# A two-layer hybrid decoder trunk in fp32r triple products: the two token halves of a projection unit computed side by side

## The chip, the cores and the metric

One Trainium2 chip, one core. The metric is the device time of one execution in microseconds; the number given for a kernel is the median of its runs.

## The reference

x is 1024 tokens by 1024 features, fp32. Two layers, then a final RMSNorm:

```python
def hybrid_layer(x, p_i, ...):
    h = rmsnorm(x, norm_mix)
    z = h @ w_in                        # 1024 x 3336: retention, pooling, mLSTM inputs
    ...                                 # y_ret, y_pool, y_ml: chunkwise mixing over tokens
    x = x + concat([y_ret, y_pool, y_ml]) @ w_out
    h = rmsnorm(x, norm_ffn)
    gu = h @ w_gate_up                  # 1024 x 5632
    x = x + (silu(gu[..., :D_FF]) * gu[..., D_FF:]) @ w_down    # D_FF = 2816
    hp = rmsnorm(x, norm_ple)
    x = x + sigmoid(hp @ w_ple_gate) * (p_i @ w_ple_proj)
    return x
```

## The kernel before

Activations are kept transposed: features on the 128 partitions in eight blocks, tokens along the free dimension in two halves of 512 (HALF), h = 0 and 1. The residual is `x`; the normed input of a projection is split into `h_hi` and `h_lo` (both fp32r), each weight tile into `w_hi` and `w_lo`, and a product is three matmuls of 128x128 by 128x512: w_hi with h_hi, w_lo with h_hi, w_hi with h_lo (`three_passes`, lines 1300 to 1302). Each `pe.matmul` loads its own stationary tile; the trace lists the loads as PEld.

The weights come in units of 128x1024 (111 per layer). SP loads a unit (512 KB) into one of two raw buffers, GpSimd splits it with two instructions (w_hi, L1285; w_lo, L1288) into a ring of three, when TensorE has reported the unit three places back as done (`unit_done`).

A narrow unit is one block of 128 outputs over all eight input blocks: two fills, one for each token half, of 8 x 3 = 24 matmuls. A wide unit (down projection and p_i @ w_ple_proj) is four blocks of 128 outputs over two input blocks: eight fills of 2 x 3 = 6 matmuls, in the order block 0 half 0, block 0 half 1, block 1 half 0 and so on. Each fill goes to the next of four PSUM banks of the tile `proj`. Before a fill TensorE waits until the bank's former content is read (`emptied`, one count for each bank), after its last matmul it increments `fill_done` or, for the unit's last fill, `unit_done` (`tell`). The other four banks (`aux`) serve the mixing work.

Readers of the fills: the input projections are scaled by rstd into SBUF (VectorE L516). In the conv stage (units 1 to 6) VectorE then runs the causal convolution (L528, L531) and row work of the mLSTM gates between the units. Output and down projections are added to x (VectorE L854, `add_fill`). In an up stage (four units: gate, up, gate, up) VectorE scales the gate unit (L866), ScalarE takes silu, VectorE scales the up unit (L873), multiplies (L878), ScalarE copies to act_hi (L1219), VectorE subtracts to act_lo (L883). Within a unit VectorE goes half 0, half 1: L873 and L878 for half 0, then for half 1, then L883 for both. The ple gate: L995, sigmoid on ScalarE, L1000, L1003 (adds to x), L442 (adds the square).

The engines' programs are fixed sequences in the order of MACRO. The FFN: up(group 0), then for each further group up(g), down(g - 1), at last down(10). So an up stage is followed by a down stage 10 times a layer. During the output projection and the last down stage VectorE also adds ScalarE's squares (L442) and makes h_lo (`low_part`, L431) for the next norm: in the output projection the eight blocks of half 0 come after fill 14, those of half 1 after fill 15; TensorE's first fill of the next unit waits for them block by block (h_ready). The rstd of the norm is applied after the projection, so it is wanted only by the readers of the fills.

Of the kernel before, what the change touches and what calls it, by code (L numbers as in the profile page):

```python
# [29 lines left out]
P = 128  # L30
D = 1024
S = 1024
HALF = 512
DEPTH = 2
KC = D // P
# [173 lines left out]
def build(nc, w_d, x_d, p_d, pos_d, const_d, par_d, early_d, out_d):  # L209
    spill_d = nc.dram_tensor("x_spill", (P, KC, S), F32, kind="Internal").ap()  # L210
    with ExitStack() as ctx:
# [1081 lines left out]
        def _(pe):  # L1293
# [30 lines left out]
            def wide(L, u, k, rhi, rlo, fills=0, units=0):  # L1324

                if k == 0:
# [4 lines left out]
                             lambda c: rhi[:, c, hs(h)], lambda c: rlo[:, c, hs(h)]), u, k)  # L1331

            def sums(L, base, i):

                for h in range(2):
                    pe.wait_ge(sq_added.sem, sq_added.at(L, base + 15 + h))
                    pe.wait_ge(aux_read(("sum", i, h)), aux_free_at(L, ("sum", i, h)))
                    for t in range(4):
                        ins = pe.matmul(aux[:, h, t:t + 1], acc[:, h, P * t:P * t + P], const[:, C_PART:C_PART + 1],
                                        start=True, stop=True)  # L1340
                    ins.then_inc(aux_done.sem, 1)
# [12 lines left out]
            with pe.Fori(0, DEPTH) as L:  # L1354
                for item in MACRO:
                    what, args = item[0], item[1:]
                    if what == "unit":
                        u = args[0]
                        for h in range(2):
                            ready = None  # L1360
# [191 lines left out]
                    elif what == "out_units":  # L1552
# [9 lines left out]
                        for m in range(2, 8):  # L1562
                            for h in range(2):
                                narrow(L, U_OUT + m, h)
                    elif what == "ffn":
                        def up(u, g, lp, first=False):
                            for f in range(4):
                                for h in range(2):
                                    ready = None
# [9 lines left out]
                        def down(u, g, lp):  # L1579
                            pe.wait_ge(act_ready.sem, act_ready.at(L, lp.acts + (4 * g + 4)))  # L1580
                            for k in range(16):
                                wide(L, u + k // 8, k % 8, ahi[:, g % 2], alo[:, g % 2], lp.fills, lp.units)

# [16 lines left out]
                    elif what == "ple_gate":  # L1600
                        for m in range(8):
                            for h in range(2):
                                ready = None
                                if m == 0:
                                    ready = lambda i, k, h=h: pe.wait_ge(h_ready.sem, h_ready.at(L, 48 + 8 * h + k + 1))
                                narrow(L, U_GATE + m, h, ready=ready)
# [135 lines left out]
```

## Time and profile before

| | |
|---|---|
| runs | 2929.11, 2934.57, 2944.49 us; median 2934.57 us |
| span of the profiled execution | 2929.3 us, mean granted TensorE clock 0.984 |
| PE (matmul) busy | 2767.3 us, 94%, 12804 matmuls |
| PEld (weight loads) busy | 2242.3 us, 77%, 12804 loads |
| DVE / ACT / POOL busy | 1572.0 us (54%) / 479.7 us (16%) / 1011.8 us (35%) |
| chain that ended last | PE 80%, DVE 11%, issue 6%, ACT 2% |
| projection matmuls, per line 1300, 1301, 1302 | 2784 from h, 704 from act, 64 from p |

How to read it: PE is TensorE, DVE is VectorE, ACT is ScalarE, POOL is GpSimd. A matmul's record (0.39 us) reaches over the start of the next one, so busy time says that TensorE is seldom idle, and start-to-start distances say how fast it goes.

### The profile page before, as it was taken

To read this page: it belongs to the slowest core of one execution; us is meant where nothing else is said; L and a number is where in the kernel's file an instruction comes from. 1 tells how busy PE (TensorE), PEld (TensorE's weight loads), DVE (VectorE), ACT (ScalarE), POOL (GpSimd) and SP (SyncE) were. 2 spreads that over 40 slices of the span, in tenths; PEclk is the share of its full clock that TensorE was granted. 3 is DMA by queue.
4 is the path that set the end of the run, shared out by engine and by line. 5 is a ranking of instruction groups with operands and counts; after the bars stand their busy time and mean duration, and the time that the engine had idled before them with its cause. 6 is when DMAs were issued, how large, how long until landed. Compare 5 with 4: busy or idle time off the path is not lost.

```text
span 2929.3 us, 34599 instructions
## 1 busy us (share of the span) xinstructions
PE 2767.3 (94%) x12804; PEld 2242.3 (77%) x12804; DVE 1572.0 (54%) x2098; ACT 479.7 (16%) x719; POOL 1011.8 (35%) x449
## 2 busy tenths in 40 slices
PE   3899999999999999999978999999999999999997
PEld 3678876778888888787866887668888878888875
DVE  5957844454334334446768677345433444433566
ACT  4020212230000000004221001142200000000232
POOL 2432311333434343344433222204343434343441
PEclk9999999999999999999989999999999999999998
DMA  5110001111111111111121001021111111111111
GB/s 188 44 37 30 30 29 65 65 44 51 43 50 43 50 50 43 50 43 44 51 95 37 30 30 37 29 80 58 44 44 50 43 50 43 50 44 49 50 42 60
DMA packets 38027, 147.49 MB, mean 50 GB/s; under 512 B 4384, under 2 KB 4640, under 8 KB 36512
## 3 DMA queue, kind: packets, MB, share of 16 engines
q1 hardware_dynamic: 31968, 116.41, 11.9%
q10 hardware_dynamic: 5952, 29.65, 2.7%
q8 instruction: 68, 1.11, 0.2%
q14 instruction: 39, 0.32, 0.0%
HBM read 132.94 MB, written 12.58 MB: 50 GB/s over the span
## 4 chain that ended last, share of the span: by engine, by line
PE 80%; DVE 11%; issue 6%; ACT 2%; DVEq 0%; ACTq 0%; DMA 0%
PE proj L1300 24%; PE proj L1302 24%; PE proj L1301 24%; DVE ml_qk L531 2%; PE aux L1532 1%; PE aux L1533 1%; DVE mix L542 1%; DVE h_lo L431 1%; PE aux L1413 1%; DVE square_sum L442 1%; DVE x L854 1%; PE aux L1445 1%; PE aux L1434 1%; PE aux L1503 1%; PE aux L1471 1%
## 5 line engine op out<-in xcount | busy, mean ns | idle before, releaser
L1300 PE MATMUL proj<-h_hi,w_hi 128*128 128x512 f32 x2784 | 1105.2, 397 | 83.8 <-DVE h_lo L431 61.3
L1301 PE MATMUL proj<-h_hi,w_lo 128*128 128x512 f32 x2784 | 1091.7, 392 | 0.0
L1302 PE MATMUL proj<-h_lo,w_hi 128*128 128x512 f32 x2784 | 1091.4, 392 | 0.0
L1285 POOL TENSOR_TENSOR w_hi<-w_raw,zero 128x1024 fp32r<-128x1024 f32 x222 | 437.8, 1972 | 1845.8 <-PE proj L1302 1839.0
L1300 PEld LDWEIGHTS proj<-h_hi,w_hi 128*128 128x128 f32 x2784 | 527.8, 190 | 200.8 <-DVE h_lo L431 62.5
L1301 PEld LDWEIGHTS proj<-h_hi,w_lo 128*128 128x128 f32 x2784 | 527.7, 190 | 110.9 <-issue 3.3
L1302 PEld LDWEIGHTS proj<-h_lo,w_hi 128*128 128x128 f32 x2784 | 527.1, 189 | 111.5
L1288 POOL TENSOR_TENSOR w_lo<-w_raw,w_hi 128x1024 fp32r<-128x1024 f32 x222 | 573.9, 2585 | 17.4
L854 DVE TENSOR_TENSOR x<-x,proj 128x512 f32<-128x512 f32 x384 | 257.5, 685 | 221.5 <-PE proj L1302 221.0
L1300 PE MATMUL proj<-act_hi,w_hi 128*128 128x512 f32 x704 | 278.2, 395 | 23.2 <-DVE x L854 23.2
L1302 PE MATMUL proj<-act_lo,w_hi 128*128 128x512 f32 x704 | 276.9, 393 | 0.0
L1301 PE MATMUL proj<-act_hi,w_lo 128*128 128x512 f32 x704 | 274.8, 390 | 0.0
L873 DVE TENSOR_TENSOR act<-proj,rstd 128x512 f32<-128x512 f32 x88 | 60.9, 692 | 372.1 <-PE proj L1302 372.1
L866 DVE TENSOR_TENSOR silu_g<-proj,rstd 128x512 f32<-128x512 f32 x88 | 60.4, 688 | 275.9 <-PE proj L1302 275.9
L1215 ACT ACTIVATE silu_g<-silu_g 128x512 f32<-128x512 f32 x88 | 55.4, 632 | 748.4 <-DVE silu_g L866 748.4
L1300 PEld LDWEIGHTS proj<-act_hi,w_hi 128*128 128x128 f32 x704 | 132.3, 188 | 58.9 <-DVE x L854 31.8
L1302 PEld LDWEIGHTS proj<-act_lo,w_hi 128*128 128x128 f32 x704 | 132.3, 188 | 29.2
L1301 PEld LDWEIGHTS proj<-act_hi,w_lo 128*128 128x128 f32 x704 | 132.2, 188 | 29.2
L883 DVE TENSOR_TENSOR act_lo<-act,act_hi 128x512 fp32r<-128x512 f32 x88 | 153.5, 1782 | 0.0
L1219 ACT ACTIVATE act_hi<-act 128x512 fp32r<-128x512 f32 x88 | 55.7, 633 | 490.5 <-DVE act L878 490.5
L1026 ACT ACTIVATE squares<-x 128x512 f32<-128x512 f32 x112 | 70.3, 631 | 257.7 <-DVE x L854 175.1
L878 DVE TENSOR_TENSOR act<-act,silu_g 128x512 f32<-128x512 f32 x88 | 107.6, 1223 | 6.1
(192 smaller groups left out, 1972.1 us busy)
## 6 DMA issues: line engine op xcount, KB each, us to landing
w_raw<-weights SPq DMA_DIRECT2D x222, 512.0 KB, 3.2
x_spill<-x ACTq DMA_DIRECT2D x2, 4096.0 KB, 12.5
x<-x_spill ACTq DMA_DIRECT2D x4, 1536.0 KB, 7.2
x<-x_in ACTq DMA_DIRECT2D x8, 512.0 KB, 11.2
out<-x ACTq DMA_DIRECT2D x16, 256.0 KB, 3.0
x<-x_spill ACTq DMA_DIRECT2D x2, 1024.0 KB, 4.9
p_raw<-p_in ACTq DMA_DIRECT2D x2, 1024.0 KB, 5.0
const<-constants ACTq DMA_DIRECT2D x1, 1241.0 KB, 16.7
```

What stands on the lines that cost most here:

```text
L531: v.scalar_tensor_tensor(dst, r[:, t:t + S], w[t], dst, ALU.mult, ALU.add).then_inc(vec_step.sem, 1)
L854: v.tensor_tensor(x[:, m, hs(h)], x[:, m, hs(h)], pbank(u, k), ALU.add).then_inc(emptied[bank(u, k)].sem, 1)
L866: v.tensor_tensor(silu_g[:, h, :], pbank(ug, h), rstd[:, h, :], ALU.mult).then_inc(emptied[bank(ug, h)].sem, 1)
L873: v.tensor_tensor(act_t[:, h, :], pbank(uu, h), rstd[:, h, :], ALU.mult).then_inc(emptied[bank(uu, h)].sem, 1)
L878: v.tensor_tensor(act_t[:, h, :], act_t[:, h, :], silu_g[:, h, :], ALU.mult).then_inc(act_made.sem, 1)
L883: v.tensor_tensor(alo[:, g % 2, f, hs(h)], act_t[:, h, :], ahi[:, g % 2, f, hs(h)].bitcast(F32), ALU.subtract).then_inc(act_ready.sem, 1)
L1026: a.activation(sqr[:, j % 2, :], x[:, c, hs(h)], ACT.Square).then_inc(sq_made.sem, 1)
L1285: g.tensor_tensor(whi[:, slot, :], w, zero1[:, 0:1].to_broadcast([P, 1024]), ALU.add).then_inc(w_hi_made, 1)
L1288: g.tensor_tensor(wlo[:, slot, :], w, whi[:, slot, :].bitcast(F32), ALU.subtract).then_inc(weights_ready.sem, 1)
L1300: pe.matmul(out, wh, rhi, start=first, stop=False)
L1301: pe.matmul(out, wl, rhi, start=False, stop=False)
L1302: return pe.matmul(out, wh, rlo, start=False, stop=final)
```

## The change

A new helper `both` computes the two token halves of one block together: for each input block w_hi is used for half 0 and for half 1, then w_lo for both, then w_hi for both with h_lo, so that consecutive matmuls write alternate banks, and each stationary tile is loaded two times running. `narrow_both` and `wide_both` wait for the weights and for both banks before the first matmul, and report both fills at the end. They take the place of `narrow` and `wide` in the whole units of the input projection from unit 2 on, output units 2 to 7, the up units (but the first two of a layer), the down units and gate units 1 to 7. All sums, their order within a bank, the number of matmuls and loads, and the programs of the other engines are as before.

```diff
+            def both(L, u, ks, outs, rhi, rlo):
+
+                last = len(ks) - 1
+                for i, (k, wk) in enumerate(ks):
+                    wh, wl = whi[:, u % RING, wk:wk + P], wlo[:, u % RING, wk:wk + P]
+                    for h in range(2):
+                        pe.matmul(outs[h], wh, rhi(k, h), start=i == 0, stop=False)
+                    for h in range(2):
+                        pe.matmul(outs[h], wl, rhi(k, h), start=False, stop=False)
+                    ends = [pe.matmul(outs[h], wh, rlo(k, h), start=False, stop=i == last) for h in range(2)]
+                return ends
+
+            def narrow_both(L, u, fills=0, units=0):
+
+                pe.wait_ge(weights_ready.sem, weights_ready.at(L, units + (u + 1)))
+                for h in range(2):
+                    pe.wait_ge(emptied[bank(u, h)].sem, free_at(L, u, h, fills))
+                ends = both(L, u, [(k, P * k) for k in range(KC)], [pbank(u, 0), pbank(u, 1)],
+                            lambda k, h: hh[:, k, hs(h)], lambda k, h: hl[:, k, hs(h)])
+                for h in range(2):
+                    tell(ends[h], u, h)
+
+            def wide_both(L, u, m, rhi, rlo, fills=0, units=0):
+
+                if m == 0:
+                    pe.wait_ge(weights_ready.sem, weights_ready.at(L, units + (u + 1)))
+                for h in range(2):
+                    pe.wait_ge(emptied[bank(u, 2 * m + h)].sem, free_at(L, u, 2 * m + h, fills))
+                ends = both(L, u, [(0, P * m), (1, HALF + P * m)], [pbank(u, 2 * m), pbank(u, 2 * m + 1)],
+                            lambda c, h: rhi[:, c, hs(h)], lambda c, h: rlo[:, c, hs(h)])
+                for h in range(2):
+                    tell(ends[h], u, 2 * m + h)
...
-                        for h in range(2):
+                        if u > U_GATES + 1:
+                            narrow_both(L, u)
+                        for h in range(2 if u <= U_GATES + 1 else 0):
...
                         for m in range(2, 8):
-                            for h in range(2):
-                                narrow(L, U_OUT + m, h)
+                            narrow_both(L, U_OUT + m)
...
                             for f in range(4):
-                                for h in range(2):
+                                if not (first and f < 2):
+                                    narrow_both(L, u + f, lp.fills, lp.units)
+                                for h in range(2 if first and f < 2 else 0):
...
-                            for k in range(16):
-                                wide(L, u + k // 8, k % 8, ahi[:, g % 2], alo[:, g % 2], lp.fills, lp.units)
+                            for m in range(8):
+                                wide_both(L, u + m // 4, m % 4, ahi[:, g % 2], alo[:, g % 2], lp.fills, lp.units)
...
                         for m in range(8):
-                            for h in range(2):
+                            if m > 0:
+                                narrow_both(L, U_GATE + m)
+                            for h in range(2 if m == 0 else 0):
```

## Rows read from the trace of the kernel before

**Rows 1.** Grouped instructions: line, engine, out<-in, shapes, count | busy us, mean ns | idle before

```profile
L1300 PE MATMUL proj<-h_hi,w_hi 128*128 128x512 f32 x2784 | 1105.2, 397 | 83.8 <-DVE h_lo L431 61.3 <-DVE conv_raw L516 22.2 <-DVE ml_v L516 0.3
```

**Rows 2.** Timeline of TensorE, narrow units: start us, duration us, engine, line, operation

```profile
1213.29 0.39 PE L1301 MATMUL proj<-h_hi,w_lo 128*128 128x512 f32 x1
1213.52 0.39 PE L1302 MATMUL proj<-h_lo,w_hi 128*128 128x512 f32 x1
1213.75 0.39 PE L1300 MATMUL proj<-h_hi,w_hi 128*128 128x512 f32 x1
```

**Rows 3.** Timeline of TensorE, last up matmul and first down fills, with weight loads

```profile
1235.28 0.39 PE L1302 MATMUL proj<-h_lo,w_hi 128*128 128x512 f32 x1
...
1236.67 0.39 PE L1302 MATMUL proj<-act_lo,w_hi 128*128 128x512 f32 x1
...
1240.56 0.19 PEld L1302 LDWEIGHTS proj<-act_lo,w_hi 128*128 128x128 f32 x1
...
1240.79 0.40 PE L1302 MATMUL proj<-act_lo,w_hi 128*128 128x512 f32 x1
...
1242.26 0.51 PE L1300 MATMUL proj<-act_hi,w_hi 128*128 128x512 f32 x1 [1.08 <-DVE x L854]
1242.37 0.19 PEld L1301 LDWEIGHTS proj<-act_hi,w_lo 128*128 128x128 f32 x1
```

**Rows 4.** TensorE: rope products; a stretch of lower clock (window row: seventh figure PEclk)

```profile
364.46 3.17 PE L1471 MATMUL aux<-ret_qkv,const 128*128 128x512 f32 x7
...
614.60:616.60 2.00, 2.00 (x6) 1.52 (x6) 2.00 (x4) 2.00 (x5) 0.00 (x0) 0.50 0.03 8
...
615.66 0.63 PE L1300 MATMUL proj<-h_hi,w_hi 128*128 128x512 f32 x1
616.08 0.63 PE L1301 MATMUL proj<-h_hi,w_lo 128*128 128x512 f32 x1
```

**Rows 5.** Waits of TensorE: waited for, us in total, times, longest us

```profile
PE proj L1300 <- DVE h_lo L431: 61.3, 4, 43.9
PE proj L1300 <- DVE x L854: 23.2, 20, 1.2
```

**Rows 6.** Timeline of VectorE and GpSimd, end of an up stage; ScalarE's L1219 grouped

```profile
1230.99 0.69 DVE L878 TENSOR_TENSOR act<-act,silu_g 128x512 f32<-128x512 f32 x1
1235.70 0.69 DVE L873 TENSOR_TENSOR act<-proj,rstd 128x512 f32<-128x512 f32 x1 [4.02 <-PE proj L1302]
1236.50 1.69 DVE L878 TENSOR_TENSOR act<-act,silu_g 128x512 f32<-128x512 f32 x1
1238.11 3.50 DVE L883 TENSOR_TENSOR act_lo<-act,act_hi 128x512 fp32r<-128x512 f32 x2
1241.53 3.12 DVE L854 TENSOR_TENSOR x<-x,proj 128x512 f32<-128x512 f32 x5
...
1235.75 1.89 POOL L1285 TENSOR_TENSOR w_hi<-w_raw,zero 128x1024 fp32r<-128x1024 f32 x1 [6.44 <-PE proj L1302]
1237.72 2.74 POOL L1288 TENSOR_TENSOR w_lo<-w_raw,w_hi 128x1024 fp32r<-128x1024 f32 x1
...
L1219 ACT ACTIVATE act_hi<-act 128x512 fp32r<-128x512 f32 x88 | 55.7, 633 | 490.5 <-DVE act L878 490.5
```

**Rows 7.** Timeline of VectorE and TensorE, end of the output projection, first layer

```profile
599.73 0.69 DVE L854 TENSOR_TENSOR x<-x,proj 128x512 f32<-128x512 f32 x1 [2.79 <-PE proj L1302]
...
601.81 9.15 DVE L431 SCALAR_TENSOR_TENSOR h_lo<-x,par,h_hi 128x512 fp32r<-128x512 f32 x8 [0.79 <-ACT h_hi L1042]
...
611.01 0.50 PE L1300 MATMUL proj<-h_hi,w_hi 128*128 128x512 f32 x1 [1.13 <-DVE h_lo L431]
```

**Rows 8.** Timeline of VectorE, ple gate of the first layer

```profile
1459.22 0.68 DVE L1000 TENSOR_TENSOR ple_t<-ple_sig,ple_in 128x512 f32<-128x512 f32 x1
```

**Rows 9.** Timeline of VectorE and TensorE, conv stage of the first layer

```profile
137.20 1.29 DVE L516 TENSOR_TENSOR conv_raw<-proj,rstd 128x512 f32<-128x512 f32 x2
...
137.95 0.80 PE L1300 MATMUL proj<-h_hi,w_hi 128*128 128x512 f32 x1 [9.69 <-DVE conv_raw L516]
```

## The prediction

> **What bounds the kernel now.** I read the grouped instructions first, then TensorE's timeline in three kinds of stretch, then the waits, then the other engines at the places where TensorE waits. TensorE runs 3 x (2784 + 704 + 64) = 10,656 projection matmuls of 128x512; one of the nine groups is shown [rows 1]. Its "mean ns of one" (397) is no cost, since they overlap: the cost is the distance from start to start. In a narrow unit the starts are 0.227 us apart (1213.29, 1213.52, 1213.75), and the pair in the middle is a change of bank: the one at 1213.52 ends a fill, the one at 1213.75 begins the next fill in the next bank, with a semaphore wait between them, and the distance is the same [rows 2]. 24 matmuls take 5.44 us, so 0.2267 us each. In a down projection, where the bank changes after every 6 matmuls, three fills end at 1236.67 to 1240.79 with 18 matmuls between the two starts: 0.2289 us each [rows 3]. 10,656 x 0.227 us is 2417 us, 82% of the span of 2929.3 us. So a change can help or harm in two ways only: the distance between matmuls, or the places where TensorE stands still.
>
> **The pace: does alternating banks or a repeated weight tile change 0.227 us?** I say no, from three rows. First, the bank: if adding to the bank just written cost anything, the one matmul that goes to another bank would come earlier; it doesn't [rows 2]. Second, the fp32 products of the rope stage: each pe.matmul of line 1471 is two records on the same bank, one behind the other, and seven records take 3.17 us with 0.59 us for the last one: (3.17 - 0.59) / 6 = 0.43 us, which is twice 512 columns at 2.4 GHz (0.4267 us) with nothing left over for the second write to the same bank [rows 4]. Third, the clock: at a granted clock of 0.50 (1.2 GHz) the same fp32r matmuls start 0.427 us apart, which is 512 columns at 1.2 GHz exactly; at 2.4 GHz 512 columns would be 0.2133 us and 0.0133 us is added [rows 4]. A toll of array cycles for the bank or for the swap of weights would be twice as long at half the clock, and there it is nil. Something that doesn't follow the array clock paces the fast stream (the feed of the moving operand is my guess), and the change leaves as many matmuls, as many columns and as many moving reads as before. The weight loads: a load starts at 1240.56, takes 0.19 us and is over before its matmul starts at 1240.79; after a pause the second load starts at 1242.37, 0.11 us behind the start of the first matmul, so a tile can be in place after 0.11 us [rows 3]. Loading the same tile twice running therefore saves nothing, even if the chip should skip the second load; and TensorE's other repeated loads, the rope matrix four products long, are all still there as records. Cost of this part: 0; the bounds are in the rivals. The Trainium skill (TensorE: Matmul & The Clock Gate, "Back-to-back issue gap") gives 512/2.4 + 2.5 = 215.8 ns for an isolated matmul; the trace has 226.7 ns. By that figure there would be 10.9 ns to win on each matmul, and the trace doesn't say that banks are what stands in the way.
>
> **What is converted.** Per layer: 11 units of the input projection (2 to 9 and U_RET to U_RET + 2), 6 output units, 42 up units, 22 down units, 7 gate units: 88, of 48 matmuls each, so 2 x 88 x 48 = 8448 matmuls. The halves interleaved with the mLSTM and retention work, the first unit of each norm stage and ple_proj stay.
>
> **What moves: two fills now end together.** Both banks must be free before the first matmul of a pair, and the first half's result comes at the end of the pair, 0.23 us ahead of the second instead of a whole fill (5.44 or 1.37 us) ahead. TensorE's own work is the same; the price is where VectorE's work on the first half used to lie beside the second half's matmuls.
>
> (a) **From up to down, 20 times.** TensorE waits there now [rows 5]: 1.16 us each by the waits, until x has been added for fill 0 of the down unit. VectorE's chain behind the last up fill (last matmul at 1235.28, [rows 3]) is: L873 1235.70, L878 1236.50 for 1.69, two L883 from 1238.11 for 3.50, five L854 from 1241.53; TensorE resumes at 1242.26 when the first is done [rows 3, 6]. The 1.69 us is not work: the same L878 took 0.69 us with GpSimd idle (1230.99); it ended 0.55 us behind GpSimd's w_hi (1235.75 + 1.89 = 1237.64), and L883 likewise behind w_lo (1237.72 + 2.74 = 1240.46) [rows 6]. So VectorE's SBUF-to-SBUF work and GpSimd take turns, and GpSimd's two instructions start with the end of the unit, before and after the change. After it, both halves' L873 and L878 stand behind that end. From 1235.48: L873 h0 to 1236.17; L878 h0 waits for w_hi, to 1238.19; L873 h1 (from PSUM, not held up in any row) to 1238.9; L878 h1 waits for w_lo, to 1241.0; ScalarE's copy of h1 takes 0.63; L883 h0 beside it, L883 h1 to 1242.35; adds 0 and 1, to 1243.6, since the third pair of banks wants both. TensorE resumes at 1243.6 instead of 1242.26, the first down pair to the second losing 0.7 us inside that same wait. Cost 1.37 us x 20 = 27.4 us. Without the lock (all of h0's L873 + L878, 1.4, less 0.23, plus one add, 0.6) it is 1.8 us; if both of h0's operations also meet GpSimd, 2.8 us; if the order of the lock turns out well, 0.7. Range 14 to 56 us. What is late next is nothing: from the third pair on VectorE has 2.75 us for two adds of 0.6 to 0.69.
>
> (b) **Output projection to the FFN norm, twice.** Fill 14 landed at 599.7; its add and then the h0 part of the norm (eight L431 from 601.81 for 9.15 us) ran beside the last fill, and TensorE waited only at the last k, until 611.01 [rows 7]. With fill 14 landing 5.44 - 0.23 = 5.2 us later the whole chain moves by 5.2 us and TensorE stands still for some 5.5 us before the first up fill. It would then drop to 1.2 GHz and start at 0.427 us a matmul, partly hidden, as one k in 0.6 to 1.1 us is all that VectorE delivers. 5.7 us each, 11.4 in all; bounds 4 and 8 each.
>
> (c) **End of each layer.** The rest of h0's chain (L995, L1000, L1003, L442, one of them 0.68 us [rows 8]) now stands behind the last fill as well: 4 x 0.68 = 2.7 us, twice, 5.5 us. The norm waits for its end with nothing beside it.
>
> (d) **Conv stage.** TensorE stood until 137.95 for the first of two evacuations (L516, 1.29 us for two, from 137.20) [rows 9]; now it needs the second too: 0.65 us, twice, 1.3 us. The stall before it in the same stage only feeds this one.
>
> (e) **Last down stage of each layer**, where VectorE adds squares as well: up to 1 us each, mostly covered by the waits for the rstd row behind it: 1.5 us. **Down stages otherwise**: half as many places where the bank changes; if the excess of 0.013 us per fill belongs to them, half of 352 x 0.013 = 2.3 us comes back.
>
> Not on the path: in the middle of an up stage VectorE needs some 7 us for a unit and has 10.9; GpSimd's weight splitting and SP's loads are released by the same unit ends as before.
>
> **Sum.** 27.4 + 11.4 + 5.5 + 1.3 + 1.5 - 2.3 = 44.8 us. The profiled execution's span is 2929.3 us, 5.3 us below the median of the runs (2934.57), so I add the sum to the median: 2979.4 us. The Trainium skill (Perfetto Trace Analysis, "Optimizing Tensor Performance", Matmuls) wants independent groups to rotate through banks, so that one is emptied while the next is computed; the rows of (a) and (b) say the same, and this change moves away from it: the two groups in flight end together.
>
> **Rivals.** *The alternate bank pays (10%).* If the 13.3 ns belong to the second write to a bank or to a changed weight tile, 8448 x 13.3 ns = 112 us go and 45 come: 2934.6 - 67 = 2867 us; with the part of it down to 215.8 ns, 2888. For it: an excess over the columns does exist. Against: [rows 2, 4]. It decides the sign as soon as the distance falls by more than 45/8448 = 5.3 ns. *The losses are mostly covered (10%).* The lock falls well in (a), and (b) is hidden behind a slower start: 2935 to 2950 us, about 2943. *The pace gets worse (22%).* The down stages run at 0.2289 us per matmul where narrow ones run at 0.2267, and no other engine explains it. If waiting more tightly or alternating operands sets that mode everywhere, 6336 narrow matmuls x 2.2 ns = 14 us are added: 2993 us; a cost of the same 13 ns per change of bank seen in the down stages, paid at every matmul, would be 110 us, 3090 us, and only the even distance in [rows 2] speaks against it (4 of the 22%). *The change does nothing* (the second load is skipped, or the order is the same to the array): that is the pace part of my forecast, and (a) to (e) still stand. The forecast itself: 58%.
>
> **How the numbers follow.** Forecast 2979, its own range 2958 to 3003 from (a) and (b). The 80% range takes in the covered case's upper part and the milder slow pace: 2943 to 3015. A difference under 0.5% (14.7 us) can't be told from none here. Faster: 11% (the bank case, a sliver). Same: 7% (most of the covered case). Slower: 82%.
>
> **What would show it.** Narrow stretches: starts 0.227 us apart in the after trace, or 0.213 to 0.216 if the bank case holds. Up to down: 20 waits of TensorE for x L854, 1.2 us before, some 3 us after with the 0.7 at the second pair. A wait of 5 to 6 us for h_lo ahead of each first up unit. TensorE's waits for h_lo L431 in total, now 61.3 us [rows 5]: some 10 us more from (b) and 2.7 from (c), whose second instance is a wait for square_sum. The forecast is wrong if the distance between matmuls moves by more than 2 ns, which is 17 us over the 8448.

## The result and the profile after

The changed kernel takes 2974.79 us, the median of four runs (2973.64 to 2976.14), against 2937.48 us for the kernel before (2929.11 to 2944.49). The ratio is 1.0126, with the interval 1.0106 to 1.0146: slower by 1.3%. The forecast was 2979 us. The spans of the two profiled executions are 2973.4 and 2929.3 us, so 44.1 us apart, at the same mean granted clock of 0.984. The kernel before scatters over 15 us from run to run and its profiled execution lies near the lower end, so it is the distance of the spans that stands beside the sum of 44.8 us. By the medians above the distance is 37.3 us, and 41.0 us against the kernel before as it ran beside the first experiments (2933.79 us, the median of 17 runs).

The page of the changed kernel, busy time by engine and one of its groups (line, shapes, count | busy us, mean ns | idle before):

```profile
span 2973.4 us, 34907 instructions
PE 2770.1 (93%) x12804; PEld 2238.2 (75%) x12804; DVE 1553.3 (52%) x2098; ACT 478.0 (16%) x719; POOL 1010.5 (34%) x449
...
L878 DVE TENSOR_TENSOR act<-act,silu_g 128x512 f32<-128x512 f32 x88 | 179.0, 2035 | 6.1
```

TensorE is busy for as long as before (2770 us against 2767), with as many matmuls and loads. What has grown is time in which it stands, and the last row points to where: the multiplication of gate and up, L878, has a mean of 2035 ns, where it was 1223 ns. Of its 88 instructions 86 now run beside one of GpSimd's, where 44 did. VectorE's own work on it is 690 ns (its duration with GpSimd idle, [rows 6]).

The pace in a narrow unit of the changed kernel. The timeline now puts the two matmuls that share a line into one record:

```profile
1229.96 0.62 PE L1339 MATMUL proj<-h_hi,w_hi 128*128 128x512 f32 x2
1230.41 0.61 PE L1341 MATMUL proj<-h_hi,w_lo 128*128 128x512 f32 x2
1230.86 0.62 PE L1342 MATMUL proj<-h_lo,w_hi 128*128 128x512 f32 x2
```

From start to start it is 0.45 us for two matmuls. From the start of a unit's last matmul to that of the next unit's, 48 matmuls, the median is 226.7 ns each in narrow units, in both kernels [rows 2], and 228.9 ns in down units that nothing holds up, in both. Alternate banks and a weight tile loaded twice running change nothing.

TensorE's waits (waited for: us in total, times, longest):

```profile
PE proj L1300 <- DVE h_lo L431: 71.9, 4, 43.6
PE proj L1339 <- DVE x L854: 38.3, 24, 1.8
PE proj L1339 <- DVE conv_raw L516: 23.6, 4, 9.7
PE proj L1339 <- DVE act L873: 11.7, 20, 0.7
```

The wait for h_lo has grown from 61.3 to 71.9 us and the one for x from 23.2 to 38.3 us [rows 5]; one kind, 20 times 0.59 us for act L873, is new. Here is one transition from an up stage to a down stage, the stretch that answers to [rows 3, 6] (start us, duration us, engine, line; in brackets the idle time before it and what ended it):

```profile
1251.26 0.62 PE L1342 MATMUL proj<-h_lo,w_hi 128*128 128x512 f32 x2
1251.69 0.69 DVE L873 TENSOR_TENSOR act<-proj,rstd 128x512 f32<-128x512 f32 x1 [9.59 <-PE proj L1342]
1251.96 1.89 POOL L1285 TENSOR_TENSOR w_hi<-w_raw,zero 128x1024 fp32r<-128x1024 f32 x1 [6.44 <-PE proj L1342]
1252.42 1.99 DVE L878 TENSOR_TENSOR act<-act,silu_g 128x512 f32<-128x512 f32 x1
1253.93 2.72 POOL L1288 TENSOR_TENSOR w_lo<-w_raw,w_hi 128x1024 fp32r<-128x1024 f32 x1
1254.33 0.68 DVE L873 TENSOR_TENSOR act<-proj,rstd 128x512 f32<-128x512 f32 x1
1255.11 2.09 DVE L878 TENSOR_TENSOR act<-act,silu_g 128x512 f32<-128x512 f32 x1
1255.15 0.71 PE L1339 MATMUL proj<-act_hi,w_hi 128*128 128x512 f32 x2 [0.50 <-DVE act L873]
1257.12 1.47 DVE L883 TENSOR_TENSOR act_lo<-act,act_hi 128x512 fp32r<-128x512 f32 x2
1258.50 2.47 DVE L854 TENSOR_TENSOR x<-x,proj 128x512 f32<-128x512 f32 x4
...
1259.93 0.71 PE L1339 MATMUL proj<-act_hi,w_hi 128*128 128x512 f32 x2 [1.74 <-DVE x L854]
```

VectorE has been idle for 9.59 us when both halves land at once; before, it had 4.02 us of idle time there and half 0 was already dealt with [rows 6]. Its two L878, 0.69 us of work each, take 1.99 and 2.09 us beside GpSimd's two instructions. TensorE stands twice: 0.50 us because the second L873 comes late, and 1.74 us because the first two additions do. It resumes at 1259.93, which is 8.44 us after the last up matmul began (1251.49, the second of the pair at 1251.26).

At the end of the output projection and at the end of a layer (answering to [rows 7] and [rows 8]):

```profile
604.78 0.69 DVE L854 TENSOR_TENSOR x<-x,proj 128x512 f32<-128x512 f32 x1 [5.19 <-PE proj L1342]
...
607.42 7.48 DVE L431 SCALAR_TENSOR_TENSOR h_lo<-x,par,h_hi 128x512 fp32r<-128x512 f32 x8
...
610.31 0.80 PE L1300 MATMUL proj<-h_hi,w_hi 128*128 128x512 f32 x1 [5.34 <-DVE h_lo L431]
...
1486.63 2.10 DVE L1000 TENSOR_TENSOR ple_t<-ple_sig,ple_in 128x512 f32<-128x512 f32 x1
...
1503.70 0.79 PE L1300 MATMUL proj<-h_hi,w_hi 128*128 128x512 f32 x1 [17.49 <-DVE h_lo L431]
```

### The profile page after: what moved, and what is told of

It is laid out like the page before. It is cut to its first block, busy times and chain, and to the rows that moved or that the text cites. A ratio compares the mean times of both kernels' runs of the same rounds, so it can differ in the third digit from the quotient of the medians.

```text
span 2973.4 us, 34907 instructions
## 1 busy us (share of the span) xinstructions
PE 2770.1 (93%) x12804; PEld 2238.2 (75%) x12804; DVE 1553.3 (52%) x2098; ACT 478.0 (16%) x719; POOL 1010.5 (34%) x449
## 4 chain that ended last, share of the span: by engine, by line
PE 79%; DVE 13%; issue 5%; ACT 2%; DVEq 0%; ACTq 0%; DMA 0%
PE proj L1339 18%; PE proj L1341 18%; PE proj L1342 18%; PE proj L1300 5%; PE proj L1301 5%; PE proj L1302 5%; DVE ml_qk L531 2%; DVE act L878 1%; PE aux L1567 1%; PE aux L1568 1%; DVE mix L542 1%; DVE act L873 1%; PE aux L1448 1%; DVE h_lo L431 1%; DVE square_sum L442 1%
## 5 line engine op out<-in xcount | busy, mean ns | idle before, releaser
L1339 PE MATMUL proj<-h_hi,w_hi 128*128 128x512 f32 x2112 | 653.3, 391 | 25.0 <-DVE conv_raw L516 23.6
L1341 PE MATMUL proj<-h_hi,w_lo 128*128 128x512 f32 x2112 | 652.0, 390 | 0.0
L1342 PE MATMUL proj<-h_lo,w_hi 128*128 128x512 f32 x2112 | 651.2, 390 | 0.0
L1341 PEld LDWEIGHTS proj<-h_hi,w_lo 128*128 128x128 f32 x2112 | 397.6, 188 | 83.1
L1342 PEld LDWEIGHTS proj<-h_lo,w_hi 128*128 128x128 f32 x2112 | 397.2, 188 | 83.2
L854 DVE TENSOR_TENSOR x<-x,proj 128x512 f32<-128x512 f32 x384 | 247.1, 682 | 250.9 <-PE proj L1342 250.0
L1300 PE MATMUL proj<-h_hi,w_hi 128*128 128x512 f32 x672 | 278.6, 415 | 71.9 <-DVE h_lo L431 71.9
L873 DVE TENSOR_TENSOR act<-proj,rstd 128x512 f32<-128x512 f32 x88 | 60.3, 685 | 406.6 <-PE proj L1342 402.9
L1339 PE MATMUL proj<-act_hi,w_hi 128*128 128x512 f32 x704 | 222.3, 397 | 50.0 <-DVE x L854 38.3
L1301 PE MATMUL proj<-h_hi,w_lo 128*128 128x512 f32 x672 | 266.0, 396 | 0.0
L1302 PE MATMUL proj<-h_lo,w_hi 128*128 128x512 f32 x672 | 265.6, 395 | 0.0
L1341 PE MATMUL proj<-act_hi,w_lo 128*128 128x512 f32 x704 | 219.4, 393 | 0.0
L1342 PE MATMUL proj<-act_lo,w_hi 128*128 128x512 f32 x704 | 218.1, 391 | 0.0
L878 DVE TENSOR_TENSOR act<-act,silu_g 128x512 f32<-128x512 f32 x88 | 179.0, 2035 | 6.1
## 6 DMA issues: line engine op xcount, KB each, us to landing
x<-x_in ACTq DMA_DIRECT2D x8, 512.0 KB, 11.4
```

Source lines behind the costliest of these rows:

```text
L854: v.tensor_tensor(x[:, m, hs(h)], x[:, m, hs(h)], pbank(u, k), ALU.add).then_inc(emptied[bank(u, k)].sem, 1)
L873: v.tensor_tensor(act_t[:, h, :], pbank(uu, h), rstd[:, h, :], ALU.mult).then_inc(emptied[bank(uu, h)].sem, 1)
L878: v.tensor_tensor(act_t[:, h, :], act_t[:, h, :], silu_g[:, h, :], ALU.mult).then_inc(act_made.sem, 1)
L1300: pe.matmul(out, wh, rhi, start=first, stop=False)
L1301: pe.matmul(out, wl, rhi, start=False, stop=False)
L1302: return pe.matmul(out, wh, rlo, start=False, stop=final)
```

## The experiments

Theory A is that the loss is lost cover: two results land together where VectorE's work on the first used to lie beside the second's matmuls, and at the transitions VectorE's SBUF work takes turns with GpSimd's. The rivals: each matmul or unit costs a little more in pair order (theory B), or a little less, hidden under larger losses (theory C).

**Does the pair order itself cost or give anything?** x3_slack is the kernel before with pairs only where nobody waits for their end: 4608 matmuls in pair order.

```diff
-                        for m in range(2, 8):
-                            for h in range(2):
-                                narrow(L, U_OUT + m, h)
+                        for m in range(2, 7):
+                            narrow_both(L, U_OUT + m)
+                        for h in range(2):
+                            narrow(L, U_OUT + 7, h)
...
-                                for h in range(2):
+                                if not (first and f < 2) and f < 3:
+                                    narrow_both(L, u + f, lp.fills, lp.units)
+                                for h in range(2 if (first and f < 2) or f == 3 else 0):
```

> The pair order only where I expect VectorE to have time: units 7 to 9 and the three of U_RET, output units 2 to 6, the first three units of each up stage, gate units 1 to 6. 48 units per layer, 4608 matmuls; down stages, last up units, the last output and gate unit and the conv units as before the change. Theory A: start to start stays 0.2267 us in pairs, nothing waits: the time of the kernel before, 2937 us, within 4. Theory C (alternate banks or repeated tiles do save something, hidden under larger losses): every ns per matmul is 4.6 us here, so 5 ns would give 2914 us. Theory B: half of the loss stays: 2957 us.

It takes 2934.98 us against 2933.79, a ratio of 0.9998 (0.9989 to 1.0006), and its pace, measured as above, is 226.7 ns.

The order of the matmuls is worth nothing either way in these narrow units, and the rivals on the pace fall. The down units are not in this run; their pace in the changed kernel (228.9 ns, as before) speaks for the same. All of the loss comes from the places left out here.

**Are the tails where the loss is?** x1_tails is the changed kernel with only the last output unit and the last gate unit back in the old order:

```diff
-                        for m in range(2, 8):
+                        for m in range(2, 7):
                             narrow_both(L, U_OUT + m)
+                        for h in range(2):
+                            narrow(L, U_OUT + 7, h)
...
-                            if m > 0:
+                            if 0 < m < 7:
                                 narrow_both(L, U_GATE + m)
-                            for h in range(2 if m == 0 else 0):
+                            for h in range(2 if m in (0, 7) else 0):
```

> The changed kernel, with output unit 7 and gate unit 7 of each layer computed half after half again (2 of its 88 converted units per layer). Theory A (the loss is VectorE's work on the first half, which stands behind the end of the unit where nothing covers it): the traces of before and after differ by 5.0 and 4.3 us at the two starts of the FFN and by 2.4 us at the end of each layer, so some 14 us of the 37 come back: 2961 us. Theory B (the pair order costs a little at each matmul or each unit, and the places are chance): 2 of 88 units are 1 us: 2974 us.

2966.88 us, 7.9 us less than the changed kernel, which lies between the two expectations. The first of its waits has lost the 11 us that the change had added, and the waits of the transitions stay:

```profile
PE proj L1300 <- DVE h_lo L431: 60.8, 4, 43.7
...
PE proj L1339 <- DVE act L873: 11.7, 20, 0.7
```

Measured by when the last matmul of each unit starts, the two ends of the output projection and the two of the layers now cost 2.6 us more than before, where in the changed kernel they cost 12.2: 9.6 us came back, and 1.2 us of this went into a later start of the whole kernel. The expectation of theory A took 14 us to be there. The place was right and its size was not. 1.6 us stay at each output end, and they are the granted clock of TensorE. Here are the 20 us around the end of the output projection in the kernel before and in the changed one (layer 0) and in x1 (layer 1); the seventh figure is PEclk:

```profile
604.00:624.00 20.00, 18.56 (x82) 14.91 (x82) 15.13 (x19) 11.20 (x18) 7.48 (x4) 0.91 0.09 27
...
604.00:624.00 20.00, 14.66 (x61) 11.81 (x60) 18.28 (x24) 13.89 (x23) 4.57 (x2) 0.83 0.08 27
...
2058.00:2078.00 20.00, 18.56 (x75) 14.80 (x74) 17.08 (x22) 13.15 (x21) 5.04 (x2) 0.83 0.08 27
```

At 0.83 eight more matmuls start 0.427 us apart (granted clock 0.50, 1.2 GHz) instead of 0.227 (2.4 GHz), which makes 1.6 us. The kernel before has 0.91 in both layers, the changed kernel 0.83 in layer 0 and 0.91 in layer 1, x1 0.83 in both. x4 (below), whose output stage is that of before, has 0.83 in layer 0 and 0.91 in layer 1. So these 1.6 us come and go with the execution, and no run ties them to the order of the matmuls.

x2_lastup does the same for the last unit of each up stage:

```diff
-                                if not (first and f < 2):
+                                if not (first and f < 2) and f < 3:
                                     narrow_both(L, u + f, lp.fills, lp.units)
-                                for h in range(2 if first and f < 2 else 0):
+                                for h in range(2 if (first and f < 2) or f == 3 else 0):
```

> The changed kernel, with only the last of the four units of each up stage computed half after half. Theory A: VectorE is done with half 0 of that unit before the unit ends, as before the change; what is left is that the third pair of down fills wants two adds instead of one, 0.6 us each time. The 20 waits cost 0.6 us instead of 1.43 us more than before the change, so 17 us come back: 2958 us. Theory B: 22 of 176 units give back an eighth of the loss, 5 us: 2970 us. If the order of GpSimd's and VectorE's turns doesn't matter, the gain is that of the uncovered L873 and L878 alone, 1.2 us x 20 = 24 us: 2951 us.

2964.70 us: 10.1 us came back where 17 were expected. The wait for act L873 is gone from its list, the one for x is not:

```profile
PE proj L1339 <- DVE x L854: 40.2, 24, 1.9
```

By the units' ends, ten transitions cost 7.5 us over the kernel before in layer 0, where 6 were expected, and 13.9 us in layer 1. The difference is the granted clock again: in layer 1 four of the ten transitions cost 2.2 to 2.3 us and the other six 0.7 us, and behind the pause of those four some eight matmuls start 0.427 us apart. The first of them, where TensorE had stood for 1.93 us before 2164.16:

```profile
2160.00:2170.00 10.00, 8.07 (x29) 6.19 (x28) 6.50 (x8) 0.07 (x1) 1.67 (x1) 0.83 0.16 52
```

At the third transition, with the same pause, the granted clock stays at 1.00 (window 2298:2308). So a transition of x2 costs 0.7 to 0.8 us over the kernel before at the full clock, 15 us for the twenty, and its profiled execution has some 6 us of lower clock on top. These 15 us fit the down pairs, where the third pair of banks wants two additions, not one; no run undoes the down pairs alone.

**What holds VectorE up: is it the turns with GpSimd?** x6_lock is the changed kernel with one thing moved: GpSimd's split that begins at the end of each up stage waits until VectorE's last L883 of that stage is done. 20 of the 222 splits are put off, and GpSimd's loop is written out for it.

```diff
+            later = {}
+            for l in range(DEPTH):
+                for grp in range(1, FG):
+                    later[l * UNITS + U_FFN + 6 * grp + 1 + RING] = (act_ready.sem, act_ready.at(l, 4 * grp + 4))
+            for n in range(DEPTH * UNITS):
...
+                if n in later:
+                    g.wait_ge(*later[n])
```

> The changed kernel; VectorE's and TensorE's programs as they are. GpSimd's split of the one weight unit that it would begin at the end of each up stage waits until VectorE has done its L883 (20 of 222 splits, each wanted only two units later); its loop is written out for that. Theory A with the lock: without GpSimd beside it VectorE needs 0.69 us for each L873 and L878, both L883 are done 4.3 us after the end of the unit and the first two adds 5.5 us after it. The first wait goes and the second goes almost: 2.5 us x 20 = 50 us back: 2925 us, even below the kernel before. Without the lock as a cause (VectorE's long instructions are slow for a reason of their own, ports of PSUM or the write to fp32r): no change, 2975 us.

2916.93 us, a ratio to the kernel before of 0.9943 (0.9926 to 0.9959). Putting GpSimd off wins 58 us and carries the pair order below the kernel before. Its transition:

```profile
1228.69 0.69 DVE L873 TENSOR_TENSOR act<-proj,rstd 128x512 f32<-128x512 f32 x1 [9.59 <-PE proj L1346]
1229.42 0.69 DVE L878 TENSOR_TENSOR act<-act,silu_g 128x512 f32<-128x512 f32 x1
1230.03 0.68 DVE L873 TENSOR_TENSOR act<-proj,rstd 128x512 f32<-128x512 f32 x1
...
1230.81 0.69 DVE L878 TENSOR_TENSOR act<-act,silu_g 128x512 f32<-128x512 f32 x1
1231.42 1.48 DVE L883 TENSOR_TENSOR act_lo<-act,act_hi 128x512 fp32r<-128x512 f32 x2
1232.81 2.67 DVE L854 TENSOR_TENSOR x<-x,proj 128x512 f32<-128x512 f32 x4
1233.07 1.89 POOL L1289 TENSOR_TENSOR w_hi<-w_raw,zero 128x1024 fp32r<-128x1024 f32 x1 [10.61 <-DVE act_lo L883]
```

Both L878 are back at 0.69 us, the additions begin 4.12 us after the first L873 (1228.69 to 1232.81) instead of 6.81 (1251.69 to 1258.50), and of TensorE's waits for L873 and for x only four for x are left, 3.0 us in all; they stand in the last down stages. These 2.7 us are the turns with GpSimd. By the units' ends the twenty transitions gave 55.4 of the 58.9 us between the two spans, and 3.2 more lie at two places of layer 0 where the execution of the changed kernel has the lower granted clock. The Trainium skill (SBUF — State Buffer, "SBUF: two separate sides") says that VectorE and GpSimd share one pair of ports, held for the whole instruction by whichever began, when VectorE's operation has two inputs in SBUF and GpSimd's reads SBUF. By that, L878 and L883 would be held up and L873, with one input in PSUM, would not; the rows agree (0.69 and 0.68 us for L873 beside GpSimd, 1.99 and 2.09 us for L878). The held L878 end 0.55 us after GpSimd's instruction, a little less than their own 0.69 us.

**Can the wait be removed in both orders from VectorE's side?** x4_defer is the kernel before, and x5_defer_pairs the changed kernel, with the two L883 of an up stage's second unit pair (act_lo, wanted only by the down stage after the next up stage) moved behind the first two additions of the down stage that runs now:

```diff
+            def act_low(L, g, f, lp):
...
+                    if g == 0 or f == 0:
+                        act_low(L, g, f, lp)
...
                     add_fill(L, uu, kk, k // 2, k % 2, 0, lp.units, lp.told)
+                    if k == 1 and late is not None:
+                        act_low(L, late, 1, lp)
```

> The kernel before, one thing moved on VectorE: in an up stage that a down stage follows, the two L883 of the second pair of units (act_lo, read only by the down stage after the next up stage) come after the first two adds of the down stage instead of ahead of them. Theory A: the 20 waits of TensorE for x L854 (1.16 us each, 1.25 us above the ordinary distance) are VectorE's queue, adds behind L883 behind GpSimd. They go, and nothing else is late in the next 16 fills, where VectorE has 1.37 us for each add of 0.69: 2937 - 25 = 2912 us. Rival: the add is late because of PSUM or the lock itself, and the wait moves to fill 6: no change, 2937 us.

> The changed kernel with the move of x4_defer: the two L883 of an up stage's second pair of units come after the first two adds of the down stage. Theory A: VectorE still has both halves' L873 and L878 behind the end of the stage, each L878 held until GpSimd's instruction ends. The first wait (for L873 of half 1, 0.6 us) stays, the second shrinks from 1.9 us to some 0.6, as two L883 with their waits are gone from it: 1.3 us x 20 = 26 us back: 2949 us, still well above x4_defer's 2902. Rival (the deferral removes all that the pairs cost in this place): 2975 - 50 = 2925 us.

x4 takes 2902.39 us (0.9884; 0.9867 to 0.9901), x5 2946.69 us (1.0043; 1.0026 to 1.0060). In x4 TensorE no longer waits for x at all: the twenty transitions are 29.0 us shorter (1.36 us each in layer 0, 1.53 in layer 1), where [rows 5] shows 1.16 us of wait each. The span is 26.8 us shorter; the granted clock takes back 1.6 us at each of two places in layer 0 and gives 1.6 us at one in layer 1. In VectorE's timeline of x4 the additions begin 2.40 us after L873 (its line 880), where it was 5.83 us ([rows 6]: 1235.70 to 1241.53), and the two L883 (line 861) follow them:

```profile
1226.97 0.69 DVE L880 TENSOR_TENSOR act<-proj,rstd 128x512 f32<-128x512 f32 x1 [4.02 <-PE proj L1308]
...
1227.76 1.69 DVE L885 TENSOR_TENSOR act<-act,silu_g 128x512 f32<-128x512 f32 x1
...
1229.37 1.27 DVE L854 TENSOR_TENSOR x<-x,proj 128x512 f32<-128x512 f32 x2
1230.57 2.32 DVE L861 TENSOR_TENSOR act_lo<-act,act_hi 128x512 fp32r<-128x512 f32 x2
```

In x5 the same move brings the transitions level with the kernel before (0.04 us each in both layers), but no further. What remains are the waits that the pair order makes:

```profile
PE proj L1345 <- DVE act L880: 11.7, 20, 0.7
PE proj L1345 <- DVE x L854: 10.9, 24, 1.0
```

With the deferral in both, the pair order costs 44.3 us (2946.69 - 2902.39), 41.0 us by the spans, about as much as it does without (37.3 by the medians, 44.1 by the spans). So it is a cost of its own, on top of the wait that this move removes.

**What are the 13.3 ns on top of the columns?** Two runs go after this, neither meant as an improvement. x7_pace is the changed kernel in which the inner blocks of an up stage's units take 256 or 384 tokens, or a stationary tile 64 columns wide, so part of the up sums is left out:

```diff
-                    wh, wl = whi[:, u % RING, wk:wk + P], wlo[:, u % RING, wk:wk + P]
+                    wh, wl = whi[:, u % RING, wk:wk + c], wlo[:, u % RING, wk:wk + c]
...
-                                    narrow_both(L, u + f, lp.fills, lp.units)
+                                    narrow_both(L, u + f, lp.fills, lp.units, cols=64 if f == 2 else P, toks=(512, 256, 512, 384)[f])
```

> The changed kernel with smaller matmuls in the middle of the up units, to see what sets 0.2267 us. In the six inner input blocks of each pair (first and last stay whole) the second unit of each up stage moves 256 token columns, the third has stationary tiles of 64 columns instead of 128, the fourth moves 384 columns; the rest of the sums is left out, so the output is not the reference's. If 13.3 ns are a fixed addition to the columns: 256/2.4 + 13.3 = 120 ns and 384/2.4 + 13.3 = 173 ns; if they are a rate, 6.25% of the columns: 113 and 170 ns. If the weight load takes part in them (16 cycles for 128 columns), the unit with 64 columns goes at 220 ns; if the load is hidden, at 227 ns.

Three stretches of it; 8, 6 and 4 matmuls lie between the two starts:

```profile
1117.75 0.40 PE L1347 MATMUL proj<-h_hi,w_lo 128*128 128x256 f32 x2
...
1118.71 0.40 PE L1348 MATMUL proj<-h_lo,w_hi 128*128 128x256 f32 x2
...
1126.75 0.63 PE L1348 MATMUL proj<-h_lo,w_hi 128*64 128x512 f32 x2
...
1128.13 0.63 PE L1348 MATMUL proj<-h_lo,w_hi 128*64 128x512 f32 x2
...
1136.88 0.51 PE L1345 MATMUL proj<-h_hi,w_hi 128*128 128x384 f32 x2
...
1137.57 0.51 PE L1348 MATMUL proj<-h_lo,w_hi 128*128 128x384 f32 x2
```

256 columns take 0.96 / 8 = 120 ns, 384 take 0.69 / 4 = 173 ns, 512 take 226.7 ns. Less the columns at 2.4 GHz (106.7, 160.0, 213.3) that is 13.3, 13 and 13.4 ns; over the whole inner part of the units (35 distances) 256 columns take 119.8 and 384 take 174.1 ns. It is one addition of 13 to 14 ns for each matmul, whatever its length. Half as many stationary columns take 1.38 / 6 = 230 ns, 3 ns more and not less, so the addition isn't time that grows with the columns of the load. The Trainium skill (TensorE: Matmul & The Clock Gate, "Back-to-back issue gap") puts an addition of 2.5 ns on an isolated matmul: 109.2 ns for 256 columns, where this kernel shows 120. It is the right form with another constant.

x8_sizes is the kernel before with two readings changed: in the inner blocks of the second up unit the matmuls take the upper half-words of the same tiles as bf16, and all down stages but a layer's last read h_hi and h_lo in place of the act tiles; both change the sums.

```diff
+                        pe.matmul(out, b(wh), b(mh), start=False, stop=False)
...
+                                    wide(L, u + k // 8, k % 8, hh[:, 0:2, :], hl[:, 0:2, :], lp.fills, lp.units)
```

> The kernel before with two readings of the pace. (1) In the second unit of each up stage but the first, the six inner input blocks are read as bf16 (the upper half of every fp32 word, so the sums are only coarse): if the 13.3 ns belong to the fp32r read of weights or tokens, these matmuls start 216 ns or less apart; if every 512-column matmul with a fresh tile has them, 227 ns. (2) The down stages but the last read h_hi and h_lo in place of act_hi and act_lo (so x gets other sums, and the output is not the reference's): if the 2 ns that a down matmul takes more come from where the act tiles lie, the down stages go at 227 ns; if they come from 6-matmul fills, they stay at 229 ns.

```profile
1204.51 0.39 PE L1318 MATMUL proj<-h_hi,w_lo 128*128 128x512 bf16 x1
...
1208.11 0.39 PE L1319 MATMUL proj<-h_lo,w_hi 128*128 128x512 bf16 x1
...
1210.20 0.39 PE L1319 MATMUL proj<-h_lo,w_hi 128*128 128x512 bf16 x1
...
1213.60 0.39 PE L1319 MATMUL proj<-h_lo,w_hi 128*128 128x512 bf16 x1
...
1253.36 0.39 PE L1300 MATMUL proj<-h_hi,w_hi 128*128 128x512 f32 x1
...
1256.08 0.39 PE L1300 MATMUL proj<-h_hi,w_hi 128*128 128x512 f32 x1
```

The bf16 stretch of half 0 has 16 matmuls in 3.60 us, 225 ns each, that of half 1 has 15 in 3.40 us, 226.7 ns each, and so it is in all these units. Neither is near 216, so the addition isn't a matter of the type fp32r (bf16 on packed data was not tried). The down stage fed from h has 12 in 2.72 us, 226.7 ns, where the act tiles gave 228.9. So the 2 ns by which down stages are slower [rows 3] come with what these matmuls read, the act tiles, not with the change of bank after every 6 matmuls. What about these tiles costs it wasn't separated.

**A version better than both.** x9_best is the kernel before with the move of x4, and with GpSimd's split put off also at the end of the output projection and of layer 0:

```diff
+                later[l * UNITS + U_OUT + 7 + RING] = (h_ready.sem, h_ready.at(l, 48))
+            later[UNITS - 1 + RING] = (h_ready.sem, h_ready.at(1, 16))
```

> The kernel before with x4_defer's move, and GpSimd's split put off at the three places where VectorE's chain is what TensorE waits for: after each up stage, after output unit 7 (until h_lo is made) and after the first layer's last gate unit (until the next layer's h_lo is made). Theory: x4_defer's 2902; the split met L431 (8 in 9.15 us instead of 5.4) with 1.3 us of waiting behind it in each layer, and L1000 and L1003 at the end of layer 0 (1.87 and 2.71 us instead of 0.69 each, 3.2 us): 2902 - 2.6 - 3.2 = 2896 us. Rival (what is put off collides later): 2902.

2895.43 us, 0.9868 (0.9851 to 0.9884) of the kernel before and 2.7% below the changed one. Both output ends gave 3.6 us instead of 1.3; some 1.6 us of each are the granted clock, which is 1.00 there in x9 (604:624 and 2022:2042) and 0.91 in the kernel before. The layer end gave 3.3 as expected; the split put off there then met the conv stage of layer 1, which lost 4.8 us at one place, 3.0 of it in a new wait, and kept 4.5 of them:

```profile
PE proj L1312 <- DVE h_lo L431: 55.5, 2, 43.8
...
PE proj L1312 <- DVE ml_v L516: 3.1, 2, 3.0
```

## Why the prediction was right, and where its terms were not

The difference of the spans by place, from the start of the last matmul of each unit in both timelines. At one place two executions of the same code can differ by 1.6 us, the lower granted clock shown at x1: x4, with the output stage and the last down stage of before, is 1.6 us later than before at each of the two in layer 0.

| place | forecast | measured |
|---|---|---|
| pace of the converted matmuls | 0 | 0 (226.7 ns in both) |
| (a) 20 transitions | 27.4 | 28.6 (14.3 in each layer) |
| (b) output projection to FFN norm | 11.4 | 8.4 (4.9 and 3.5) |
| (c) ends of the layers | 5.5 | 3.8 (1.5 and 2.3) |
| (d) conv stage | 1.3 | 0.0 (+0.4 and -0.4) |
| (e) last down stages, squares | 1.5 | 3.9 (3.6 and 0.3) |
| other down stages | -2.3 | 0 |
| start of the kernel | | -0.6 |
| sum | 44.8 | 44.1 |

**The pace** was argued from the even distance across a change of bank, from the fp32 products and from the lower clock [rows 2, 4]. All three rows held, and x3 shows the result apart from the rest. The guess beside them, that the feed of the moving operand sets the pace, isn't shown: by x7 the addition is the same for 256 and for 512 columns, so it isn't a slower feed of each column.

**(a)** is right in mechanism and size. The chain written out from 1235.48 said that TensorE resumes at 1243.6, so 8.32 us after the last up matmul of [rows 3] began; it was 8.44 after the last pair. Each step is in the timeline: L878 of half 0 held until w_hi is done, L873 of half 1 not held, L878 of half 1 held until w_lo is done. One detail was off: I had the 0.7 us lost ahead of the second down pair, and it is 0.50, for the second L873. The two waits, 2.24 us, are 1.16 more than the 1.08 of before, and 1.43 are measured. From start to start the one pause of before takes 1.24 us more than the usual distance and the matmul behind it 0.11; the two pauses of the changed kernel take 0.67 and 1.90, and the matmuls behind them 0.08 each. So each pause costs some 0.25 us more than the list of waits has for it, and now there are two. x6 shows that 2.7 of the roughly 6.8 us of the chain are turns with GpSimd, and x5 that moving L883 does not save the pair order.

**(b)** came as the predicted wait: 5.34 us where "some 5.5" stood. The term was mis-sized by the eight L431, which I moved unchanged with their 9.15 us [rows 7]. Coming 5 us later they meet less of GpSimd's work: one of them is held (2.84 us) where two were (2.38 and 2.86 us), and the eight take 7.48 us. The shift of 5.2 us less the 1.67 us saved is 3.5 us. Against x4, whose output stage is that of before, the two places cost 3.3 and 3.5 us, so the true size is nearer 7 than 8.4; the rest is the lower granted clock of layer 0. A duration that contains waiting for another engine doesn't move with the instruction. The same error, the other way round, is in (c): 0.68 us each were taken from [rows 8], but the shown L1000 takes 2.10 us beside GpSimd; that the end of the layer nevertheless cost less than forecast suggests that not all four operations lie on the path, which no run separates.

**(d)** held at the place itself: the stall before the unit grew by 0.69 us. But by the output units 0.3 us of it were made up again in layer 0, and all of it and 0.4 us more in layer 1, where the mixing work follows. Part of the latter is the granted clock: over 80 us of that stage it is 0.87 before and 0.91 after in layer 1 (1556:1636, 1580:1660), where it is 0.91 in both in layer 0. x1 (0.89 there), with the same conv stage, comes out 0.15 us above the kernel before there. The step that failed is that a stall of the conv stage was taken as lost for good.

**(e)** was half of what it should be. Against x4, whose last down stage is that of before, the two layers cost 2.0 us each. The uneven 3.6 and 0.3 are the granted clock behind the last down stage, in the second unit of p_i @ w_ple_proj: in layer 0 it is 1.00 before and 0.91 after (1358:1378, 1379:1399), in layer 1 0.91 before and 1.00 after (2796:2816, 2839:2859). In the prediction "up to 1 us each, mostly covered" is wrong, since TensorE waits there twice in each layer, as the 3.0 us left in x6 show. The gain of 2.3 us "if the excess of 0.013 us per fill belongs to" the change of bank did not come, and x8 shows why: the excess comes with the act tiles.

That the sum fits to 0.7 us is luck: the misses are -3.0, -1.7, -1.3, +2.4, +2.3, +1.2 and -0.6, the granted clock of the two executions moves single places by 1.6 us, and by the medians the distance is 37.3 or 41.0 us. The mechanism carries the result, since (a) alone is 28.6 of 44.1 us. The two expectations after it missed by more (14 and 17 us for x1 and x2, 8 and 10 measured): that for x1 read 5.0 us and twice 2.4 us where 3.3, 1.5 and 2.3 are the pair order's, and in x2 a transition still costs 0.7 to 0.8 us over the kernel before where 0.6 was taken, with the lower clock at four of them on top.

## What to carry to other kernels

Before two groups of matmuls are made to advance together, look at who reads them: the first result then lands with the second, and every reader that used to work beside the second group stands behind its end. Count that cost at each place where TensorE waits for those readers, with the reader's duration beside the engine it takes turns with, not its duration alone. Where TensorE waits at the end of a stage, look on VectorE's queue for work that only a later stage wants, and on GpSimd's for instructions that can begin a few microseconds later: here the first gave 31 us and both together 37 us, while the order of the matmuls gave nothing.

## What the runs showed of the hardware

- An fp32r matmul with a fresh stationary tile each takes its columns at 2.4 GHz and 13 to 14 ns more, for 256, 384 and 512 columns alike (120, 173 to 174 and 226.7 ns), and no addition at a granted clock of 0.50 (0.427 us, [rows 4]). Bank order, a tile loaded twice running, the width of the tile (64 columns, 230 ns) and bf16 readings with a step of two (225 and 226.7 ns) all leave it nearly as it is. What it is stays open.
- The place or content of the moving tiles is worth 2 ns a matmul: 228.9 ns from the act tiles, 226.7 from the h tiles in the same stage.
- A VectorE operation with two inputs in SBUF that meets a GpSimd instruction ends about 0.55 us after that instruction, instead of after its own 0.69 us (0.545 to 0.56 us for the 130 held L878 and 46 held L883 of both kernels); one with an input in PSUM isn't held (at most 0.69 us for the 130 L873 and 290 L854 beside GpSimd). Putting GpSimd off at twenty places was worth 58 us in the changed kernel, more than the whole change costs.
- Executions of the same code differ in where TensorE's granted clock drops to 0.50 behind a pause: at four of ten like transitions of x2, and in some executions at the end of the output projection and in the second ple_proj unit. Each such drop is some eight matmuls at 0.427 instead of 0.227 us, 1.6 us, as large as the cost of a transition. A difference at one place can be read only beside PEclk at that place in both traces.
